# Projecting the values of three attention branches with tokens stationary and weight columns moving

## The reference

```
h = h + 0.5 * swiglu_1(rmsnorm(h))
u = rmsnorm(h);  z = u @ w_in        # q, k, v of branches a, b, c; forget logits; gates
o_a = differential attention, 4 heads of values 128 wide, rmsnorm of the output
o_b = forgetting attention, 8 heads of 64      # softmax(q k / 8 + c_q - c_k) v
o_c = stick-breaking attention, 8 heads of 64
m = sum_i sigmoid(gate_i) * (o_i @ proj_i);  h = h + m @ w_out
h = h + 0.5 * swiglu_2(rmsnorm(h))
```

## Time and profile before

| | us |
|---|---|
| median of 3 runs | 2438.66 |
| lowest, highest | 2438.55, 2438.97 |
| the profiled execution | 2438.91 |
| its span in the trace | 2437.1 |

### The profile page before, as it was taken

One profiled execution on the slowest core, in us unless ns is written; L12 is line 12 of the kernel. 1 busy time (PEld: TensorE's weight loads), 2 busy tenths in 40 slices (PEclk: granted clock), 3 DMA queues, 4 the chain that ended last, 5 costly groups with the idle time before them and its releaser, 6 DMA issues.

```text
span 2437.1 us, 48108 instructions
## 1 busy us (share of the span) xinstructions
PE 2425.9 (100%) x15514; PEld 2210.7 (91%) x15514; DVE 2130.1 (87%) x3960; ACT 1493.9 (61%) x2917; POOL 4.0 (0%) x14
## 2 busy tenths in 40 slices
PE   9999999999999999999999999999999999999999
PEld 7999888888899889998889998888888998899988
DVE  8999878998898779998699997789998986899985
ACT  7666357888754456664366664578886554566643
POOL 0000000000000000000000000000000000000000
PEclk9999999999999999999999999999999999999999
DMA  4333332212232323233333323322212333233332
GB/s 168 108 103 104 113 97 69 77 55 78 62 113 79 112 87 105 104 106 117 102 103 106 103 95 106 103 79 61 72 60 70 105 106 102 87 107 104 117 113 78
DMA packets 64676, 233.72 MB, mean 96 GB/s; under 512 B 7168, under 2 KB 7552, under 8 KB 64512
## 3 DMA queue, kind: packets, MB, share of 16 engines
q1 hardware_dynamic: 64368, 231.58, 29.3%
q10 hardware_dynamic: 144, 0.10, 0.0%
HBM read 229.55 MB, written 2.10 MB: 95 GB/s over the span
## 4 chain that ended last, share of the span: by engine, by line
PE 94%; DVE 3%; ACT 1%; issue 1%; DMA 0%; DVEq 0%; SPq 0%; ACTq 0%
PE ps L715 29%; PE ps L717 29%; PE ps L716 29%; PE ps L988 2%; PE ps L1031 1%; PE ps L978 1%; PE ps L979 1%; PE ps L1030 1%; DVE w_lo L1990 1%; ACT w_hi L1293 0%; PE ps L994 0%; PE ps L1042 0%; PE ps L1043 0%; DMA h<-x 0%; DVE u_lo L1990 0%
## 5 line engine op out<-in xcount | busy, mean ns | idle before, releaser
L1293 ACT ACTIVATE w_hi<-w_raw 128x512 fp32r<-128x512 f32 (+1 forms) x874 | 624.1, 721 | 470.6 <-PE ps L717 231.3
L1990 DVE TENSOR_TENSOR w_lo<-w_raw,w_hi 128x512 fp32r<-128x512 f32 (+1 forms) x874 | 699.2, 805 | 108.2 <-ACT w_hi L1293 91.8
L715 PE MATMUL ps<-u_hi,w_hi 128*128 128x256 f32 (+1 forms) x2432 | 786.1, 323 | 0.6 <-DVE w_lo L1990 0.6
L717 PE MATMUL ps<-u_hi,w_lo 128*128 128x256 f32 (+1 forms) x2432 | 781.0, 321 | 0.0
L716 PE MATMUL ps<-u_lo,w_hi 128*128 128x256 f32 (+1 forms) x2432 | 780.2, 321 | 0.0
L716 PE MATMUL ps<-area,w_hi 128*128 128x256 f32 (+1 forms) x1778 | 583.4, 328 | 0.0
L715 PEld LDWEIGHTS ps<-u_hi,w_hi 128*128 128x128 f32 x2432 | 463.3, 190 | 37.4 <-issue 2.3
L717 PEld LDWEIGHTS ps<-u_hi,w_lo 128*128 128x128 f32 x2432 | 463.2, 190 | 35.1
L716 PEld LDWEIGHTS ps<-u_lo,w_hi 128*128 128x128 f32 x2432 | 463.5, 191 | 32.8
L715 PE MATMUL ps<-area,w_hi 128*128 128x512 f32 (+1 forms) x1414 | 482.0, 341 | 2.4 <-ACT scratch_whole L1392 1.8
L717 PE MATMUL ps<-area,w_lo 128*128 128x512 f32 (+1 forms) x1414 | 480.1, 340 | 0.0
(11 more groups left out here) (220 smaller groups left out, 2909.4 us busy)
## 6 DMA issues: line engine op xcount, KB each, us to landing
w_raw<-weights SPq DMA_DIRECT2D x432, 512.0 KB, 3.7
h<-x SPq DMA_DIRECT2D x4, 512.0 KB, 6.4
out<-scratch_whole SPq DMA_DIRECT2D x8, 256.0 KB, 2.0
scratch_whole<-const_b SPq DMA_DIRECT2D x1, 512.0 KB, 9.6
scratch_whole<-const_r SPq DMA_DIRECT2D x1, 192.0 KB, 8.9
cst<-const SPq DMA_DIRECT2D x1, 137.0 KB, 8.0
par<-params ACTq DMA_DIRECT2D x1, 98.0 KB, 4.5
```

Source lines behind the costliest of these rows:

```text
L715: pe.matmul(dst, hi, x_hi, start=start, stop=False, **kw)
L717: return pe.matmul(dst, lo, x_hi, start=False, stop=stop, **kw)
L1293: return act.activation(dst, src, ACT.Copy)
L1990: return dve.tensor_tensor(dst, src, hi_part.bitcast(F32), ALU.subtract)
```

## The change

The values of all three branches are made together, with the tokens stationary. The three v units of a tile stand in the stream of weights one after the other behind q and k of branch c, laid out so that each of the eight blocks of inputs has 384 columns side by side (a, b, c). `value_steps` goes through 32 steps: eight blocks of inputs for token blocks 0 and 1, then eight for token blocks 2 and 3. A step is three products of 128x384 into a part of a bank. Where the columns wrap around the end of the slots (k == 2), the step is six products, three of 128x256 and three of 128x128. All three slots stay in use through both passes; `unit_done` comes at steps 21, 27 and 31. The result has tokens in partitions, so `take` and `turn_values` are not needed for values: `values_hi` and `values_lo` read the bank, multiply by `token_rstd` (a column per token block) and write the parts. `token_rstd` is `rstd` turned once a layer (`turn_rstd`, four transposes, and a small ACT copy). Units of q and k change slots and banks; those of b and a now come after the values, in the order q b, k b, q a, k a. The values of a tile are written where the outputs of the same tile will stand.

```diff
+            def value_steps(begin, end, before):
+
+                for n in range(begin, end):
+                    late, m = divmod(n, 2 * UNIT)
+                    k, j = m // 2, 2 * late + m % 2
+                    if n == 0:
+                        pe.wait_ge(staged, c.next(staged, 2 if before else 1))
+                    elif n == 2 * UNIT:
+                        pe.wait_ge(staged, c.next(staged))
+                    elif n == 2 * UNIT + 1 and before:
+                        pe.wait_ge(v_set, c.next(v_set))
+                    at = k * SEQ + j * P
+                    x_hi, x_lo = u_hi[:, at:at + P], u_lo[:, at:at + P]
+                    for first, after in ((0, 2), (2, 3)) if k == 2 else ((0, 3),):
+                        if (n, first) in ((0, 0), (4, 2), (10, 0)):
+                            pe.wait_ge(w_set, c.next(w_set))
+                        b = (2 * UNIT + 3 * k + first) % (SLOTS * UNIT)
+                        of = slice(b * P, (b + after - first) * P)
+                        dst = ps[:, val_banks(before)[j], first * P:after * P]
+                        pe.matmul(dst, x_hi, w_hi[:, of], start=k == 0, stop=False, skip_group_check=True)
+                        pe.matmul(dst, x_lo, w_hi[:, of], start=False, stop=False, skip_group_check=True)
+                        last = pe.matmul(dst, x_hi, w_lo[:, of], start=False, stop=k == UNIT - 1, skip_group_check=True)
+                        if (k, j, first) in ((2, 3, 0), (5, 3, 0), (7, 3, 0)):
+                            last.then_inc(unit_done, 1)
+                    if k == UNIT - 1 and j < 3:
+                        last.then_inc(v_mm, 1)
...
-            def weighted(branch, hd, before=True):
-
-                if hd == 0:
-                    pe.wait_ge(v_set, c.next(v_set))
+            def weighted(t, branch, hd, before=True):
+
+                if (branch, hd) == (2, 0):
+                    pe.wait_ge(v_set, c.next(v_set, 2))
...
-                unit(0)
+            def bank_read(n=1):
+
+                pe.wait_ge(staged, c.next(staged, n))
+
+            def rest_of_tile(t, unit, known=1):
+
+                if known:
+                    bank_read(known)
+                unit(0, 0)
                 turn_probs(1)
-                turn_values(0)
-                unit(1, 0, 3)
-                weighted(1, 1)
+                bank_read()
+                unit(1, 1, 0, 3)
+                weighted(t, 1, 1)
                 scores(0, 0)
-                unit(1, 3, 7)
+                unit(1, 1, 3, 7)
                 scores(0, 1)
-                unit(1, 7)
+                unit(1, 1, 7)
                 c.skip(max_set, NQ)
 
-            def heads(before):
+            def heads(t, before):
 
                 if before:
-                    rest_of_tile(unit)
-                    unit(2)
+                    rest_of_tile(t - 1, unit, 1 if t > 1 else 0)
+                    value_steps(0, 12, before)
                     turn_probs(0)
-                    unit(3, 0, 3)
-                    weighted_whole()
-                    unit(3, 3, 5)
+                    value_steps(12, 16, before)
+                    weighted_whole(t - 1)
+                    value_steps(16, 19, before)
                 else:
-                    unit(0, first=True, before=False)
...
+                    unit(1, 1, 3)
+                    turn_rstd()
+                    value_steps(0, 11, before)
                     pe.wait_ge(pads_set, c.next(pads_set, 4))
+                    pe.wait_ge(token_rstd_set, c.next(token_rstd_set))
                 stick_scores(0)
                 if before:
-                    unit(3, 5, 6)
+                    value_steps(19, 20, before)
+                    pe.wait_ge(v_set, c.next(v_set))
                     diff_norm()
-                unit(3, 6 if before else 0)
-                unit(4, 0, 6)
+                value_steps(20 if before else 11, 30, before)
+                turn_probs(0)
+                value_steps(30, 32, before)
                 if before:
                     pe.wait_ge(o_rstd, c.next(o_rstd))
-                turn_values(0)
+                else:
+                    pe.wait_ge(v_set, c.next(v_set, 2))
+                own = (AUX, 0, 1, AUX) if before else (0, AUX, 1, AUX)
+                unit(own[0], 2, 0, 5)
+                weighted(t, 2, 0, before)
+                stick_scores(1)
+                unit(own[0], 2, 5)
+                unit(own[1], 0)
                 turn_probs(0)
-                unit(4, 6)
-                unit(5, 0, 4)
-                weighted(2, 0, before)
-                stick_scores(1)
-                unit(5, 4)
-                unit(6, 0, 7)
+                unit(own[2], 1, 0, 5)
+                weighted(t, 2, 1)
+                scores(1, 0)
+                unit(own[2], 1, 5)
+                bank_read(1 if before else 2)
+                unit(own[3], 2, 0, 3)
                 turn_probs(0)
-                unit(6, 7)
-                unit(7, 0, 4)
-                weighted(2, 1)
-                scores(1, 0)
-                unit(7, 4)
-                unit(8, 0, 2)
-                turn_probs(0)
-                turn_values(1)
-                unit(8, 2)
-                weighted(1, 0)
+                unit(own[3], 2, 3)
+                weighted(t, 1, 0)
                 scores(1, 1)
                 c.skip(max_set, 2 * NQ)
...
-            def values_hi(branch):
-                act.wait_ge(turned, c.next(turned))
-                if branch == 0:
-                    hi(val(0, 0), ps[:, AUX, :]).then_inc(v_hi_set, 1)
+            def values_hi(t, j, before):
+
+                if j < 3:
+                    act.wait_ge(v_mm, c.next(v_mm))
                 else:
-                    for hd in range(2):
-                        hi(half_val(branch, hd, 0), half_tile(hd)).then_inc(v_hi_set, 1)
+                    act.wait_ge(unit_done, c.peek(unit_done))
+                if (t, j) == (0, 0):
+                    act.wait_ge(token_rstd_set, c.next(token_rstd_set))
+                of, scale = ps[:, val_banks(before)[j], :], token_rstd[:, j:j + 1]
+                act.activation(val_block(t, 0, 0, j), of[:, 0:P], ACT.Copy, scale=scale)
+                act.activation(val_parts(t, j, 0), of[:, P:3 * P].rearrange("p (b n) -> p b n", n=HEAD), ACT.Copy,
+                               scale=scale).then_inc(v_hi_set, 1)
...
-                values_hi(2)
                 turned_hi(0)
                 turned_hi(1)
                 turned_hi(2)
                 turned_hi(3)
+                values_hi(t, 2, before)
+                values_hi(t, 3, before)
                 split(1)
-                qk_hi(1, 0, 3, 2)
                 if before:
                     act.preload_act_table(ACT.Sigmoid)
                 output_rest(0)
@@ -1731,12 +1771,13 @@
                 stick_sigmoids(2)
                 stick_sigmoids(3)
                 act.preload_act_table_set(LN_EXP)
-                qk_hi(1, 2, 4)
+                qk_hi(1, 0, 0)
                 split(2)
                 turned_hi(0)
                 turned_hi(1)
                 turned_hi(2)
                 turned_hi(3)
+                qk_hi(1, 2, 1)
                 split(0)
                 output_rest(1)
                 output_hi(2, t)
@@ -1749,9 +1790,8 @@
                 turned_hi(1)
                 turned_hi(2)
                 turned_hi(3)
-                values_hi(1)
-                qk_hi(0, 0, 6, 2)
-                qk_hi(0, 2, 7)
+                qk_hi(0, 0, 0)
+                qk_hi(0, 2, 1)
...
+                take(1, 1, 1.0, first=True)
+                split(1)
...
-            def take(k, scale):
-
-                if k >= 2:
+            def take(k, bank, scale, first=False):
+
+                if not first:
                     dve.wait_ge(qk_set, c.peek(qk_set, 0))
                 dve.wait_ge(unit_done, c.next(unit_done))
-                dve.scalar_tensor_tensor(tile(k % 2), ps[:, k % 2, :], scale, rstd[:], ALU.mult, ALU.mult
...
+                dve.scalar_tensor_tensor(tile(k), ps[:, bank, :], scale, rstd[:], ALU.mult, ALU.mult).then_inc(staged, 1)
...
-            def values_lo(branch):
-                if branch == 0:
...
+            def values_lo(t, j, before):
+
+                if (t, j) == (0, 0):
+                    dve.wait_ge(token_rstd_set, c.next(token_rstd_set))
+                dve.wait_ge(v_hi_set, c.next(v_hi_set))
+                of, scale = ps[:, val_banks(before)[j], :], token_rstd[:, j:j + 1]
+                dve.scalar_tensor_tensor(val_block(t, 0, 1, j), of[:, 0:P], scale, val_block(t, 0, 0, j).bitcast(F32),
+                                         ALU.mult, ALU.subtract)
+                dve.scalar_tensor_tensor(val_parts(t, j, 1), of[:, P:3 * P].rearrange("p (b n) -> p b n", n=HEAD), scale,
+                                         val_parts(t, j, 0).bitcast(F32), ALU.mult, ALU.subtract).then_inc(v_set, 1)
...
                     rest_of_tile(t, layer, take)
```

(37 more changed lines are left out.)

158 lines of the change are left out of this document (71 added, 87 removed).

## The result

The changed kernel takes 2527.2 us (median of 6 runs, 2526.1 to 2528.6) against 2438.6 for the kernel before, a ratio of 1.0364 with a 95% interval of 1.0353 to 1.0375. It is slower by 88.5 us. The forecast was 2527, in a range of 2500 to 2545.

The account below looks back on a forecast made before the run. TensorE, busy 100% of the span, was taken as the bound. Products -2, turn_rstd +1, first-head wait +58, second head +10, smaller waits +3, clock +19 make +89 on 2438.9: 2527.5, about 2527 us for the median; range 2500 to 2545.

Parts of the forecast that it names:

- The wait at `scores(1,0)`: First head of branch b: TensorE waits 7.3 us a tile for qk_lo of k, 58 us in eight tiles.
- The sum from `take` of q on: DVE and ACT steps in written order, from take of q to qk_lo of k ahead of scores(1,0): 15.9 us.
- The clock: After each wait at scores(1,0), the next 4.7 us of work run at half clock, 2.35 longer: 19 us.
- The second head of branch b: weighted(1,1) starts at 17.0 where 15.8 was free: 1.2 us a tile, 10 us in all.
- Smaller waits: weighted(2,0) waits behind slot 2's late release: 0.2 us in six tiles, 0.8 in two, 3 us.
- Products: Products of values take 17.4 us a tile, 1.1 more; removed transposes save 1.3: net -0.25 a tile, -2 us.
- rival (2): Products of 128 columns run at the float32 rate, 0.21 us each: 2537 us; chance 0.18.
- (1): Rival: the clock holds through the 7 us waits at scores(1,0): 2509 us; chance 0.17.
- (3): Rival: the chain ahead of scores(1,0) is shorter, half the wait, 3.6 us: 2480 us; chance 0.07.
- (4): Rival: q and k are rounded in time for scores(1,0), only the products are left: 2438 us; chance 0.05.
- (5): Rival: more stalls than were found, behind a TensorE that restarts late: above 2545 us; chance 0.08.

Follow-up runs that it names:

- the last reordered kernel: Last of successive reorderings of the changed kernel: in a layer's last tile differences and exponentials moved ahead, and one projection block put ahead of turn_probs(0); 2439.6 us.
- two of the reordered kernels: Changed kernel reordered through branch b's second head, 2454.0 us; later also turned_lo between two qk_lo and a projection block ahead of scores(1,0), 2447.2 us.

## Why the prediction was right

Point by point, with what the changed kernel and the experiments measured beside each term.

- **The wait at `scores(1,0)`: forecast 7.3 us, PE idle for 7.0, 58 us in all.** Measured from the `turn_probs` ahead, at 485.70, to the first score, at 498.90, it is 13.2 us, in each of the eight tiles, where 5.8 were free: 7.4, or 59.3 in all. Of that, 7.13 - 0.12 = 7.0 are the wait itself, 6.85 of it idle, and 0.4 the late start of `weighted(2,1)`. The sum from `take` of q on was right to 0.2 us in 16.1.
- **The clock: forecast 19, measured 13.6 in the trace and 13.9 between the medians.** This term was mis-sized. That the clock would fall in each wait was right. The step that was off is "the next 4.7 us of TensorE's work": that number came from the start of the program. In the tiles it was 3.3 to 4.7 us, 30.0 in all, 3.7 on the mean. And the cost of it was taken as a half, where 13.6 of 30.0 is 0.45.
- **The second head of branch b: forecast 1.2 us a tile.** In the changed kernel the ten transposes lose 0.45 us and the nine products between them and `weighted(1,1)` take 0.8 more (2.94 against 2.15). That is 1.24 a tile, 9.9 us.
- **Smaller waits: forecast 0.2 in six tiles and 0.8 in two, 3 us.** `weighted(2,0)` starts 0.35 late in six tiles and 0.85 in two: 3.8 us. Its row in the table of waits has 2.7, since it counts the idle part alone.
- **Products: forecast -0.25 us a tile.** In the timeline of PE, the step in which the columns wrap around, once with 256 and 128 columns and the start of the next:

```profile
450.48 0.28 PE L1032 MATMUL ps<-w_hi,u_hi 128*128 128x256 f32 x1
...
450.84 0.22 PE L1032 MATMUL ps<-w_hi,u_hi 128*128 128x128 f32 x1
450.89 0.28 PE L1033 MATMUL ps<-w_hi,u_lo 128*128 128x128 f32 x1
451.01 0.27 PE L1034 MATMUL ps<-w_lo,u_hi 128*128 128x128 f32 x1
451.12 0.33 PE L1032 MATMUL ps<-w_hi,u_hi 128*128 128x256 f32 x1
451.29 0.28 PE L1033 MATMUL ps<-w_hi,u_lo 128*128 128x256 f32 x1
```

  Three products of 128 columns take 451.12 - 450.84 = 0.28 us, against 0.33 forecast with the transpose's price and 0.64 in the rival (2) of the float32 rate. So the nearest row was the right one to take. All products of values of a tile take 17.6 us (sum of the spacings in a tile of the last reordered kernel), 17.4 were forecast. The products that are gone took 16.6 by the same count, not 16.3, so the two errors cancel; the transposes were 1.3. Net -0.3 a tile, -2.2 in all.
- **The sum.** 59.3 + 13.6 + 9.9 + 3.8 - 2.2 + 0.8 (`turn_rstd`: 0.4 us twice) = 85.2. What no term had: the products of `weighted(1,1)` and `weighted(2,0)`, once started, take 0.1 us more, 1.6 in all, and `stick_scores(0)` of a layer's first tile costs 0.4 more, twice. That makes 87.6, against 87.7 between the two profiled spans and 88.5 between the medians. The forecast's +89 is this close by luck in part: a clock rated 5 too high stood against 1.3 too little for the wait and some 3 for waits and restarts that were sized too low or left out.

The rivals. (1) and (2) are refuted as said. (3), half the wait, would have shown 3.6 us of idle time, and there are 6.85. (4), that the cover holds, was named as needing "an order other than the one written", and that is what the last of the kernels has: 2439.6 against the 2438 given for it. (5) did not happen in the changed kernel. Its mechanism, though, a wait that comes back one consumer later, is what two of the reordered kernels met.

The Trainium skill, "TensorE: Matmul & The Clock Gate", section "HAM oscillation", says that gaps without products send the clock to half rate and that each burst after them begins cold, at a penalty of half the throttled time. This trace agrees on the fall: the granted clock is 0.50 in the second part of the idle time and after it, and the kernel that fills the wait, with a clock of 1.00, is 13.9 us faster. The price is a little lower here: the work after the restarts is 30.0 us at half clock, whose half is 15.0, and it costs 13.6 by the traces.

## What to carry to other kernels

When TensorE is at 100%, a change that moves operands between units can be decided, as here, by the two engines that prepare those operands: write their queues down in order, from the last event that is fixed to the operand that is wanted, and add the durations from rows of the same kernel. Look above all for a step that waits for the other engine (here `split`) standing ahead of one that somebody needs; moving such steps, and the takes with them, added no work and gave back 69 of 88 us. Price a stall of 5 or 7 us, as here, with its clock as well, and after each repair look at the table of waits again, since the time may only have gone to the next consumer.

## What was not expected of the hardware

- A shorter idle time can cost more clock than a longer one: waits of 5.0 us were followed by 2.9 to 6.0 us of work at half clock (37.6 in eight), waits of 6.9 us by 3.3 to 4.7 (30.0 in eight), each kernel in its one profiled execution. Between the medians, the shorter wait still costs 2.1 us more for the clock than the longer one. The length of the wait alone doesn't give the price.
- The first of three products of 128 columns behind products of 256 costs only 0.05 us (450.84 to 450.89), the next two 0.12 and 0.11. The product of 256 columns that follows then takes 0.17 instead of 0.12 (451.12 to 451.29), so most of what was saved is paid back: such a mixed step of six products takes 0.64 to 0.69 us against 0.52 for three of 384.
- Added transposes cost 0.11 us each where they stand, but only 0.083 each in the whole program (8.0 us for 96).
